# Two products of a blockwise triangular inverse, cut from 64 to 32 moving columns

## What is computed

```python
def step(S, inp):
    r_t, w_t, k_t, v_t, a_t, b_t = inp
    sa = jnp.einsum('bhvk,bhk->bhv', S, a_t)
    S = S * w_t[:, :, None, :] + sa[..., None] * b_t[:, :, None, :] + v_t[..., None] * k_t[:, :, None, :]
    y = jnp.einsum('bhvk,bhk->bhv', S, r_t)
    return S, y
```

## Time and profile before

| | |
|---|---|
| median of 3 runs | 2103.09 us (2102.45 to 2104.31) |
| the profiled execution, its own time | 2099.98 us |
| its span, first to last instruction | 2098.2 us |
| TensorE clock granted, mean over the span | 0.985 |
| TensorE busy | 1995.7 us (95%) |
| VectorE, ScalarE, GpSimd busy | 1176.8, 782.9, 146.1 us |

### The profile page before, as it was taken

One profiled execution on the slowest core, in us unless ns is written; L12 is line 12 of the kernel. 1 busy time (PEld: TensorE's weight loads), 2 busy tenths in 40 slices (PEclk: granted clock), 3 DMA queues, 4 the chain that ended last, 5 costly groups with the idle time before them and its releaser, 6 DMA issues.

```text
span 2098.2 us, 34740 instructions
## 1 busy us (share of the span) xinstructions
PE 1995.7 (95%) x14160; PEld 1577.6 (75%) x14160; DVE 1176.8 (56%) x1777; ACT 782.9 (37%) x1361; POOL 146.1 (7%) x116
## 2 busy tenths in 40 slices
PE   7999999979999999999999999999999959999996
PEld 1577799968787877776777787877886738888884
DVE  5489766666544344467485746576563265556324
ACT  5786433334322222337532212235242224444211
POOL 0000132210202022000002202020000000000000
PEclk9999999989999999999999999999999979999998
DMA  5221000032233232220244453634520212232421
GB/s 186 103 91 51 1 4 4 9 138 91 91 102 99 90 97 83 92 92 31 94 167 141 141 180 130 210 122 162 153 89 10 71 69 92 96 100 84 151 80 40
DMA packets 60713, 201.37 MB, mean 96 GB/s; under 512 B 7968, under 2 KB 10912, under 8 KB 59296
## 3 DMA queue, kind: packets, MB, share of 16 engines
q1 hardware_dynamic: 59808, 192.86, 27.6%
q10 hardware_dynamic: 768, 6.55, 1.0%
HBM read 190.61 MB, written 6.42 MB: 94 GB/s over the span
## 4 chain that ended last, share of the span: by engine, by line
PE 70%; issue 17%; DVE 7%; ACT 2%; POOL 2%; SPq 1%; DMA 1%; DVEq 0%; ACTq 0%; POOLq 0%
PE bank L1868 17%; PE bank L1869 16%; PE bank L1870 16%; POOL HS L2559 2%; PE bank L2016 1%; PE bank L2038 1%; PE bank L2053 1%; PE bank L1863 1%; PE bank L2020 1%; DVE HR L1490 1%; DVE GBZ L1311 1%; PE bank L2299 1%; PE bank L2285 1%; PE bank L2320 1%; PE bank L2430 1%
## 5 line engine op out<-in xcount | busy, mean ns | idle before, releaser
L1161 DVE TENSOR_TENSOR wlo<-raw,whi 128x1024 fp32r<-128x1024 f32 x270 | 327.6, 1223 | 590.5 <-ACT whi L668 589.0
L668 ACT ACTIVATE whi<-raw 128x1024 fp32r<-128x1024 f32 x270 | 282.3, 1056 | 735.7 <-PE bank L1870 706.1
L1868 PE MATMUL bank<-inh,whi 128*128 128x512 f32 x1200 | 472.5, 394 | 19.4 <-DVEq L1803 16.1
L1869 PE MATMUL bank<-inl,whi 128*128 128x512 f32 x1200 | 468.9, 391 | 0.0
L1870 PE MATMUL bank<-inh,wlo 128*128 128x512 f32 x1200 | 468.7, 391 | 0.0
L1868 PEld LDWEIGHTS bank<-inh,whi 128*128 128x128 f32 x1200 | 226.5, 189 | 77.2 <-DVEq L1803 17.0
L1869 PEld LDWEIGHTS bank<-inl,whi 128*128 128x128 f32 x1200 | 226.6, 189 | 47.3 <-issue 1.0
L1870 PEld LDWEIGHTS bank<-inh,wlo 128*128 128x128 f32 x1200 | 226.4, 189 | 47.5
L1868 PE MATMUL bank<-hidh,whi 128*128 128x512 f32 x576 | 228.6, 397 | 14.7 <-DVE hidl L1466 8.1
L1870 PE MATMUL bank<-hidh,wlo 128*128 128x512 f32 x576 | 224.4, 390 | 0.0
L1869 PE MATMUL bank<-hidl,whi 128*128 128x512 f32 x576 | 224.4, 390 | 0.0
(11 more groups left out here) (361 smaller groups left out, 2769.8 us busy)
## 6 DMA issues: line engine op xcount, KB each, us to landing
raw<-in_mlp_w SPq DMA_DIRECT2D x128, 512.0 KB, 3.6
ADW<-in_w_ada SPq DMA_DIRECT2D x32, 768.0 KB, 4.8
raw<-in_w_up SPq DMA_DIRECT2D x44, 512.0 KB, 3.5
raw<-in_w_in SPq DMA_DIRECT2D x28, 512.0 KB, 3.6
raw<-in_a_w_rkv SPq DMA_DIRECT2D x24, 512.0 KB, 3.3
raw<-in_w_down SPq DMA_DIRECT2D x22, 512.0 KB, 3.5
raw<-in_a_wo SPq DMA_DIRECT2D x8, 512.0 KB, 8.3
raw<-in_b_wq SPq DMA_DIRECT2D x8, 512.0 KB, 3.2
```

The lines of the kernel that those rows point to most:

```text
L668: act.activation(whi[u % SLOTS][:, :], raw[u % SLOTS][:, :], ACT.Copy).then_inc(w_hi, 1)
L1161: dve.tensor_tensor(lo[:, :], r[:, :], h[:, :].bitcast(F32), ALU.subtract).then_inc(w_lo, 1)
L1868: pe.matmul(o, w[:, wc], xh, start=start, stop=False)
L1869: pe.matmul(o, w[:, wc], xl_, start=False, stop=False)
```

## The change

A level merges two neighbouring blocks. Of `z`, only the block under the diagonal of each pair is new, and it stands in half of the columns in the layout used here: the columns of the later half of each pair, which hold 32 of the 64. The changed kernel moves only these 32 columns through q, the copy, the z product and the addition. `later(z, lv)` picks them (runs of 2, 4, 8, 16 and 32 neighbouring columns in the five levels, each followed by a gap of the same length), and q writes them densely into the first half of the bank. The stationary operands, the transposition, the masks, the number of instructions, their order and their waits stay as they are.

```diff
-        QS = [at(f"QS{x}", 72 + 2 * x, [CB, HC]) for x in range(2)]
+        QS = [at(f"QS{x}", 72 + 2 * x, [CB, HC // 2]) for x in range(2)]
...
+        def later(z, lv):
+
+            w = 2 << lv
+            return z.rearrange("p a (b two w) -> p a b two w", two=2, w=w)[:, :, :, 1, :]
+
+        def merged(bank, lv):
+
+            return bank[:, 0:CB * HC // 2].rearrange("p (a b w) -> p a b w", a=CB, w=2 << lv)
+
+        def half_tok(j):
+            return slice(j * HC // 2, (j + 1) * HC // 2)
...
-                        act.activation(QS[x][:], pairs(PB[x][:]), ACT.Copy).then_inc(ai.sem, ai.step(("q", g, lv, x)))
+                        act.activation(QS[x][:], pairs(PB[x][:, 0:CB * HC // 2]), ACT.Copy).then_inc(ai.sem, ai.step(("q", g, lv, x)))
...
-                        dve.tensor_tensor(z, z, pairs(PB[2 + x][:]), ALU.add).then_inc(di.sem, di.step(("z", g, lv, x)))
+                        dve.tensor_tensor(later(z, lv), later(z, lv), merged(PB[2 + x], lv), ALU.add).then_inc(di.sem, di.step(("z", g, lv, x)))
...
-                                mm = pe.matmul(PB[x][hs, tok(cb)], LM[x][lv % 2][hs, cb, :], GBZ[j % 4][hs, cb, HC:P], start=True, stop=True)
+                                mm = pe.matmul(PB[x][hs, half_tok(cb)], LM[x][lv % 2][hs, cb, :], later(GBZ[j % 4][hs, cb:cb + 1, HC:P], lv)[:, 0], start=True, stop=True)
...
-                                mm = pe.matmul(PB[2 + x][hs, tok(cb)], TI[x][hs, cb, :], QS[x][hs, cb, :], start=True, stop=True)
+                                mm = pe.matmul(PB[2 + x][hs, half_tok(cb)], TI[x][hs, cb, :], QS[x][hs, cb, :], start=True, stop=True)
```

## The result

| | before | after |
|---|---|---|
| median | 2103.38 us (2101.65 to 2105.25, 20 runs) | 2107.53 us (2105.45 to 2109.53, 20 runs) |
| the profiled execution, its own time | 2099.98 us | 2109.25 us |
| its span | 2098.2 us | 2107.5 us |
| its mean granted clock | 0.985 | 0.977 |

The ratio is 1.0019, with a 95% interval of 1.0012 to 1.0026: slower by 4.2 us, where 9.2 us less was forecast. Not one of the 20 runs after is as quick as the slowest run before. All 20 had a mean granted clock of 0.976 to 0.979; in the 64 runs of the kernel before that stand beside the experiments it was 0.983 to 0.987. The two profiled executions lie further apart than the medians (9.3 us): the one before is 3.4 us quicker than its median, the one after 1.7 us slower.

A forecast was written before the change was run, and what follows sets the result against it. TensorE, busy 95%, bounds the kernel, with waits for VectorE at level changes. Level savings of 8.8 us, 0.1 for the rest and 0.3 for the last addition give 9.2: 2103.1 - 9.2 = 2093.9 us, range 2086.5 to 2099.0.

The forecast's parts named there:

- Where the time goes in a level: Inverse: a level's four batches would become TensorE-bound, 3.72 to 3.74 us for 4.27; first inverse 18.2 to 18.8 us.
- Additions and copies: VectorE additions 0.69 to 0.42 us, two in each level's chain; copies 598 to 378 ns, off the chain, costed at nothing.
- the rival in which the additions don't shrink: VectorE pays for each short run, so additions keep up to 0.69 us; 2102.6 us in total, chance 0.10.
- Matmuls: q and z product: a batch of 32 matmuls stays near 0.935 us, taken as 0.93, because weight loads do not shrink.
- The batches of 0.80 and 0.52 in the rivals: Loads no limit, chance 0.13: batches of 0.80 give 2087.0 us (0.09), batches of 0.52 give 2074.5 us (0.04).
- Their bound there was 0.89: q and z product: weight loads of 64 columns, two halves taking turns, 0.0278 us each, bound a batch at 0.89 us.
- The slower rival: TensorE reads q's runs of 2 and 4 columns slowly in the first two levels; 4.2 us loss or more, chance 0.05.
- There the granted clock is 1.00: Windows of the recurrence before the change: clock at full speed; no term of the sum has a clock change.
- what follows the last inverse merely moves up: What comes after the recurrence starts when it ends, and moves up with it.
- the 2.1 that the sum counted there: Each group's inverse: four level changes at 0.53 us of TensorE waiting for VectorE, 2.10 us, expected to go.
- DMA moves next to nothing: Windows of the recurrence before the change: hardly any DMA traffic; no size of saving or loss attached.
- the 8.5 us in the sum: All inverses: 16 level changes, four in each of four groups, each saving 0.53 us.

## Why the prediction was wrong

- **Where the time goes in a level: right.** TensorE became the bound, 3.73 us for four batches (3.72 to 3.74 forecast), the first inverse took 18.77 us (18.2 to 18.8).
- **Additions and copies: right.** 0.41 and 0.38 us for 0.42 and 0.38. Runs of two columns cost nothing: the additions lie between 382 and 423 ns in all levels. That answers the rival in which the additions don't shrink. The Trainium skill (Advanced Engine Details and Errata, SBUF Cachelines) asks for at least two hits on a 16-byte line, which runs of two fp32 columns just give, and the rows agree.
- **Matmuls: the time right, the reason not shown.** A batch is 0.934 us and nothing was gained by 32 columns. The batches of 0.80 and 0.52 in the rivals did not come: the level is 3.73, the same as with 64 moving columns. That the weight loads are what holds the pace stays an argument from the earlier trace rows. Their bound there was 0.89, 5% below what was measured, and no run changed the stationary columns, so a fixed cost for each matmul instruction would fit as well.
- **The slower rival: right in sign, wrong in mechanism.** In the first group the two q batches take 1.84 to 1.87 us in every level, so the runs of 2 and 4 columns cost TensorE nothing. That the change was slower after all, which had a chance of 0.05, came by another way.
- **The step that failed** is the one that isn't in the sum: "There the granted clock is 1.00". The prediction took over the clock of the kernel before in every term, put a change of it at nothing without a reason, and held that what follows the last inverse merely moves up. The change halves the columns that stream through TensorE, and with narrow products the clock fell at interruptions through which it held, or soon came back, with wide ones. In the profiled run that cost the last inverse 8.2 us instead of saving the 2.1 that the sum counted there, and its recurrence 1.2. Narrow additions with wide products gave 7.0 of the 9.2 us; the other 11.2 us of the miss lie in the narrow products with their copy, which were expected to bring next to nothing. None of the rivals had this mechanism.
- **What the prediction read past.** "DMA moves next to nothing" fits the first two windows of the earlier trace rows; the third, 180 us long, shows a DMA share of 0.10, and that mean hides the burst of up to 396 GB/s in the last inverse.
- **The size of the gain without the clock**: 7.0, not 8.8 to 11.8. The last inverse took 24.2 us as before even with wide products (2.1 of the 8.5 us in the sum were counted there). There the pauses of the burst and a short fall of the clock took what the additions save. The prediction did not read in the trace of before that this inverse took 24.15 us where the first took 20.80.
- **Recurrences**: 15.1 to 17.3 us in both kernels and in all variants where no loads were moved into them. The kernel before with late loads, whose TensorE work up to the last inverse is the old one, had 16.20, 15.65 and 16.76 with pauses of its own, 1.8 us more in sum than the profile before. So most of the 2.9 us is seen without the change; the rest one profile for each kernel can't settle.

What stays open: why fewer moving columns make the clock fall more easily, of which the runs show only that it is so; why the clock fell in a few executions without a burst; and what TensorE lacks in the burst. It pauses without a releaser, the pauses shrink when the loads are spread, and its instructions come by DMA as well; that they are late was not measured.

## What to carry to other kernels

Before a matmul is made narrower, ask what else sets its pace: here 64 and 32 moving columns went at the same 29.2 ns for each instruction, so narrowing saved nothing on TensorE, and the whole gain came from the VectorE edit alone. Then check the granted clock as a quantity of its own, in the stage with the longest interruption and not in the first one that looks the same: 31 us at 1.2 GHz, most of them in one of four like stages, cost more than the other three gave. If the clock is at stake, keep the products wide where that costs no time. Don't let large transfers land in one burst beside dense small matmuls; to move the burst as a whole did not help here, to spread it did.

## What the runs showed of the hardware

- Two matmul streams with 32 and with 64 moving columns had the same pace at full clock (1.87 us for 64 instructions), but not the same clock: after a wait of 0.93 to 0.96 us it stayed at 1.00 with 64 and went to 0.50 with 32. With 64, pauses of 1.66 and 1.93 us passed without a fall; after others of 1.93 and 2.75 us the clock was low for some 3 us. With 32, it fell after a pause of 0.50 us, and once with no wait above 0.39 us.
- At the low clock narrow matmuls alone did not bring the clock back in any of four stretches, though TensorE was busy 10.00 of 10.00 us in one of them; the pace there was 1.705 us for a batch, 1.82 times 0.935. With one product of two at 64 columns it was back in some 10 us, with both in some 3.
- The profile calls TensorE fully busy at the low level (10.00 of 10.00 us at 0.50) as well as at full clock (12.00 of 12.00 us at 1.00), so its busy row does not tell which level is granted; the clock column does.
- A VectorE copy of 128x256 fp32 took 295 ns in the median, and up to 1368 beside a running GpSimd operation; an addition that reads a bank did not show this (382 to 423 ns).
